# A two-layer encoder step with Strassen-style products: the seam reordered, scalings and squares spread, other final banks, and low halves made five steps ahead

## What is computed

```python
def swiglu(x, g, w_gate, w_up, w_down):
    n = rms_norm(x, g)
    return (jax.nn.silu(n @ w_gate) * (n @ w_up)) @ w_down
...
xp = xp + mix_output(o_a, o_lat, w_uv[l], gn_a[l], gn_b[l], w_out[l])
xp = xp + swiglu(xp, ffn_norm[l], w_gate[l], w_up[l], w_down[l])
...
y_prompt = rms_norm(xp, final_norm)
```

## Time and profile before

| | us |
|---|---|
| median of 3 executions | 1423.65 |
| lowest, highest | 1423.54, 1425.45 |
| the profiled execution | 1426.02 |
| its span, first to last instruction | 1424.7 |

### The profile page before, as it was taken

How to read it: one execution, slowest core, us unless ns; L and a number is a source line. 1 busy time by engine, 2 the same in 40 slices (tenths; PEclk the granted TensorE clock), 3 DMA queues, 4 the chain that set the end, 5 groups by cost and what they waited for, 6 DMA issues and landing times.

```text
span 1424.7 us, 24573 instructions
## 1 busy us (share of the span) xinstructions
PE 1395.9 (98%) x9278; PEld 1313.8 (92%) x9278; DVE 1118.9 (79%) x2032; ACT 737.8 (52%) x1490; POOL 157.6 (11%) x109
## 2 busy tenths in 40 slices
PE   7998999999999999999999999999999999999998
PEld 6887878999999999999988878699999999999998
DVE  5658667878789989988955776677787898988986
ACT  5459555334455455455555675633434544544555
POOL 3415020210000000000062241002000000000002
PEclk9999999999999999999999999999999999999999
DMA  5340221233022222322233211213221223222222
GB/s 172 110 116 12 74 71 35 85 104 104 30 89 66 89 85 74 104 90 75 75 99 108 71 56 47 77 45 119 60 75 60 82 79 107 78 71 90 89 68 97
DMA packets 142372, 115.27 MB, mean 81 GB/s; under 512 B 17808, under 2 KB 136976, under 8 KB 142224
## 3 DMA queue, kind: packets, MB, share of 16 engines
q1 hardware_dynamic: 142256, 113.71, 26.1%
HBM read 108.90 MB, written 6.62 MB: 81 GB/s over the span
## 4 chain that ended last, share of the span: by engine, by line
PE 84%; DVE 8%; ACT 3%; issue 2%; DMA 2%; SPq 1%; DVEq 0%; ACTq 0%
PE ps L692 18%; PE ps L1375 14%; PE ps L1376 14%; PE ps L1377 14%; PE ps L818 3%; PE ps L820 3%; PE ps L819 3%; PE ps L1252 1%; PE ps L1143 1%; ACT pw L1511 1%; DMA wraw<-w_uq 1%; PE ps L742 1%; DVE ringl L2536 1%; PE ps L933 1%; PE ps L1169 1%
## 5 line engine op out<-in xcount | busy, mean ns | idle before, releaser
L1881 ACT ACTIVATE ringh<-sums 128x512 fp32r<-128x512 f32 (+1 forms) x240 | 140.7, 586 | 130.3 <-DVE sums L2527 52.1
L1376 PE MATMUL ps<-tl,ringh 128*128 128x320 f32 x576 | 178.1, 309 | 0.0
L1375 PE MATMUL ps<-tth,ringh 128*128 128x320 f32 x576 | 177.3, 308 | 0.0
L1377 PE MATMUL ps<-tth,ringl 128*128 128x320 f32 x576 | 177.2, 308 | 0.0
L1375 PE MATMUL ps<-dhi,ringh 128*128 128x320 f32 x504 | 158.4, 314 | 6.7 <-DVE xT L2571 3.7
L2536 DVE TENSOR_TENSOR ringl<-sums,ringh 128x512 fp32r<-128x512 f32 (+1 forms) x240 | 152.7, 636 | 7.7 <-ACT ringh L1881 6.4
L1377 PE MATMUL ps<-dhi,ringl 128*128 128x320 f32 x504 | 156.4, 310 | 0.0
L2067 DVE TENSOR_TENSOR wlo<-wraw,whi 128x1024 fp32r<-128x1024 f32 (+1 forms) x69 | 79.6, 1154 | 78.1 <-ACT whi L1463 78.0
L1376 PE MATMUL ps<-dlo_rest,ringh 128*128 128x320 f32 x432 | 134.2, 311 | 0.0
L1376 PE MATMUL ps<-tbl,ringh 128*128 128x320 f32 x432 | 133.5, 309 | 0.0
L1377 PE MATMUL ps<-tbh,ringl 128*128 128x320 f32 x432 | 133.4, 309 | 0.0
(11 more groups left out here) (430 smaller groups left out, 3748.8 us busy)
## 6 DMA issues: line engine op xcount, KB each, us to landing
raw_gate<-w_gate SPq DMA_DIRECT2D x18, 1024.0 KB, 5.4
raw_up<-w_up SPq DMA_DIRECT2D x18, 1024.0 KB, 5.4
raw_gate<-w_down SPq DMA_DIRECT2D x12, 768.0 KB, 4.2
raw_up<-w_down SPq DMA_DIRECT2D x12, 768.0 KB, 4.2
wraw<-w_out SPq DMA_DIRECT2D x32, 128.0 KB, 2.9
wraw<-w_out SPq DMA_DIRECT2D x16, 256.0 KB, 3.1
wraw<-w_gate SPq DMA_DIRECT2D x8, 512.0 KB, 3.8
wraw<-w_up SPq DMA_DIRECT2D x8, 512.0 KB, 3.8
```

Source lines behind the costliest of these rows:

```text
L1375: mm(o, wh[:, c, :], xh[:, c, :], start=fresh and c == 0, stop=False, skip_group_check=True)
L1376: mm(o, wh[:, c, :], xl[:, c, :], start=False, stop=False, skip_group_check=True)
L1377: ins = mm(o, wl[:, c, :], xh[:, c, :], start=False, stop=c == (DP if down else KH) - 1, skip_group_check=True)
L1881: run(ring_of(n, x)[0], left_of(n, x), ACT.Copy).then_inc(a_hi.sem, 1)
```

## The change

Five edits, listed here as the diff has them:

- the first down group of each block runs its products in the order 1, 5, 4, 6, 3, 7, 2 instead of 1, 5, 4, 6, 3, 2, 7; its ScalarE copies `k1` and `k5` are written ahead of the right-hand pieces of the last up group (under that group's product 7), `k2s` under its product 4; the pair of pieces 5 to 7 is made as two pieces, so that there are seven pieces and not six;
- the scalings and squares of the last layer are spread over products 6, 3, 2, 7 of a group (two of them and then two more under 6 and 2 in the last group);
- other banks for the final turns and sums, and half of the turns of tile 2 ahead of the last two products;
- `AHEAD` is 5 instead of 4; `HIGH_AHEAD` stays 5 and `RING` stays 6.

```diff
-AHEAD = 4
+AHEAD = 5
 HIGH_AHEAD = 5
 RING = 6
...
-        for x in (3, 2, 7) if n < NG + NDOWN - 1 else (2, 7, 4, 3):
+        for x in (3, 7, 2) if n == first else (3, 2, 7) if n < NG + NDOWN - 1 else (2, 7, 4, 3):
...
-RIGHT_COUNT = {1: 1, 5: 2, 6: 3, 3: 4, 2: 5, 7: 6, 4: 6}
+RIGHT_COUNT = {1: 1, 5: 2, 6: 3, 3: 4, 7: 5, 2: 6, 4: 7}
...
-        return (6, 0, 4, 6, 0)[t]
+    def y_bank(t, right=0):
+        return ((6, 7), (0, 1), (2, 4), (6, 7), (0, 1))[t][right]
...
                     y_turn(1, range(4))
+                    y_turn(2, range(4))
...
-        y_turn(2, range(8)).then_inc(tile_turned.sem, 1)
+        y_turn(2, range(4, 8)).then_inc(tile_turned.sem, 1)
...
+            def down_copied(n, x):
+                bx, by, bz = group_banks(n)
+                gate_last = GROUPS_OF[(n - NG) // KH + 1][1] - 1
+                act.wait_ge(a_used.sem, a_used.at(l, STEP[n, x] + 1))
+                act.wait_ge(c_new.sem, c_new.at(l, C_NEW[gate_last, {1: 2, 5: 7, 6: 3}[x]]))
+                out, bank = {1: (k1, bx), 5: (k5, by), 6: (k2s, bx)}[x]
+                run(out[:, :], ps[:, bank, 0:HALF], ACT.Copy).then_inc(kept.sem, 1)
...
                     elif x == 7 and final:
+                        down_copied(NG + KH * (n // 6), 1)
+                        down_copied(NG + KH * (n // 6), 5)
                         down_right_hi(pair, 2, 3, t12[:, 1:2, :], right_new, sums + 2)
                         down_right_hi(pair, 4, 5, tu[:, 1:2, half(1)], right_new, sums + 2)
+                        down_right_hi(pair, 5, 6, t34[:, 0:1, :], right_new, sums + 3)
                     elif x == 7:
                         down_right_hi(pair, 1, 3, t12[:, :, :], right_new, sums + 1)
                     elif final:
+                        down_copied(NG + KH * (n // 6), 6)
                         down_right_hi(pair, 3, 4, tu[:, 1:2, half(0)], up_c21, pair + 1)
-                        down_right_hi(pair, 5, 7, t34[:, :, :], right_new, sums + 3)
+                        down_right_hi(pair, 6, 7, t34[:, 1:2, :], right_new, sums + 4)
...
-                if x == 6 and n > NG + 2 * KH:
-                    for c in (2 * (n - NG - 2 * KH) - 2, 2 * (n - NG - 2 * KH) - 1):
-                        if l == DEPTH - 1:
-                            gained(c)
-                            squared(c)
+                if n > NG + 2 * KH and l == DEPTH - 1:
+                    c = 2 * (n - NG - 2 * KH) - 2
+                    if x == 6:
+                        gained(c)
+                    elif x == (3 if n < NG + NDOWN - 1 else 2):
+                        squared(c)
+                        if n == NG + NDOWN - 1:
+                            gained(c + 1)
+                            squared(c + 1)
+                    elif x == 2:
+                        gained(c + 1)
+                    elif x == 7 and n < NG + NDOWN - 1:
+                        squared(c + 1)
...
                 elif g == 0 and x == 5:
                     down_right_lo(q, 4, 4, 5, tu[:, 1:2, half(1)])
+                    down_right_lo(q, 5, 5, 6, t34[:, 0:1, :])
                 elif g == 0 and x == 6:
-                    down_right_lo(q, 6, 5, 7, t34[:, :, :])
+                    down_right_lo(q, 7, 6, 7, t34[:, 1:2, :])
```

More of the change, by code:

```diff
@@ L153 @@
 RIGHT_OF = {1: 0, 5: 1, 6: 2, 2: 3, 3: 4, 7: 5, 4: 6}
-RIGHT_COUNT = {1: 1, 5: 2, 6: 3, 3: 4, 2: 5, 7: 6, 4: 6}
+RIGHT_COUNT = {1: 1, 5: 2, 6: 3, 3: 4, 7: 5, 2: 6, 4: 7}
 def pieces_before(pair):
-    return 4 * pair + pair // DP * 2
+    return 4 * pair + pair // DP * 3
 def right_sums_before(pair):
-    return 2 * KH + 2 * pair + pair // DP
+    return 2 * KH + 2 * pair + pair // DP * 2
 def row_done(d):
@@ L507, in scores_bank @@
         return 5 if n < 2 else 2 * (n % 2)
-    def y_bank(t):
-        return (6, 0, 4, 6, 0)[t]
+    def y_bank(t, right=0):
+        return ((6, 7), (0, 1), (2, 4), (6, 7), (0, 1))[t][right]
     def x_turn_bank(t, right):
@@ L704, in y_turn @@
             for c in chunks:
-                ins = turn(ps[:, y_bank(t) + c // 4, (c % 4) * P:(c % 4 + 1) * P], yT[:, c, tok(t)], ident)
+                ins = turn(ps[:, y_bank(t, c // 4), (c % 4) * P:(c % 4 + 1) * P], yT[:, c, tok(t)], ident)
             return ins
@@ L1420, in square_sums @@
             return ins
+        pe.wait_ge(d_new.sem, d_new.at(DEPTH, -1))
         pe.wait_ge(n_hi.sem, n_hi.at(DEPTH, 0))
@@ L1428, in _ @@
         for t in range(2):
-            ins = square_sums(2, t, [ssq, sq[:, 0], sq[:, 1]])
+            ins = square_sums(3, t, [ssq, sq[:, 0], sq[:, 1]])
         ins.then_inc(stat_sum.sem, 1)
@@ L1432, in _ @@
         for t in range(2, NT):
-            ins = square_sums(3, t, [ssq, sq[:, 0], sq[:, 1]])
+            ins = square_sums(5, t, [ssq, sq[:, 1], sq[:, 0]])
         ins.then_inc(stat_sum.sem, 1)
@@ L1892, in emptied @@
                 if n >= NG:
[L1893 to L1898, removed]
                     return
@@ L2047, in _ @@
         act.wait_ge(stat_sum.sem, stat_sum.at(DEPTH, 1))
-        run(sd[:, 0:2], ps[:, 2, 0:2], ACT.Sqrt, bias=eps, scale=1.0 / D).then_inc(stat_sd.sem, 1)
+        run(sd[:, 0:2], ps[:, 3, 0:2], ACT.Sqrt, bias=eps, scale=1.0 / D).then_inc(stat_sd.sem, 1)
         act.wait_ge(stat_r.sem, stat_r.at(DEPTH, 1))
@@ L2052, in _ @@
         act.wait_ge(stat_sum.sem, stat_sum.at(DEPTH, 2))
-        run(sd[:, 2:NT], ps[:, 3, 2:NT], ACT.Sqrt, bias=eps, scale=1.0 / D).then_inc(stat_sd.sem, 1)
+        run(sd[:, 2:NT], ps[:, 5, 2:NT], ACT.Sqrt, bias=eps, scale=1.0 / D).then_inc(stat_sd.sem, 1)
         act.wait_ge(stat_r.sem, stat_r.at(DEPTH, 2))
@@ L2581, in down_emptied @@
                     down_right_lo(q, 4, 4, 5, tu[:, 1:2, half(1)])
+                    down_right_lo(q, 5, 5, 6, t34[:, 0:1, :])
                 elif g == 0 and x == 6:
-                    down_right_lo(q, 6, 5, 7, t34[:, :, :])
+                    down_right_lo(q, 7, 6, 7, t34[:, 1:2, :])
             def first_rights(n, x):
                 if n >= NG and (n - NG) % KH == 0 and x == 6:
-                    down_right_lo(DP * ((n - NG) // KH) + DP - 1, 5, 3, 4, tu[:, 1:2, half(0)])
+                    down_right_lo(DP * ((n - NG) // KH) + DP - 1, 6, 3, 4, tu[:, 1:2, half(0)])
                 elif n < NG and n % 2 and x == 7:
@@ L2653, in emptied @@
                         vec.tensor_tensor(t12[:, 1, :], tu[:, 1, half(1)], t12[:, 0, :], ALU.subtract).then_inc(right_new.sem, 1)
-                        vec.tensor_tensor(t34[:, 0, :], tu[:, 1, half(1)], tu[:, 0, half(1)], ALU.subtract)
+                        t3 = vec.tensor_tensor(t34[:, 0, :], tu[:, 1, half(1)], tu[:, 0, half(1)], ALU.subtract)
+                        if final:
+                            t3.then_inc(right_new.sem, 1)
                 elif x == 4 and up:
@@ L2660, in emptied @@
                     vec.tensor_tensor(tu[:, 1, half(0)], ps[:, bx, 0:HALF], tg[:, 1, half(0)], ALU.mult).then_inc(up_c21.sem, 1)
-                    dve.wait_ge(right_new.sem, right_new.at(l, right_sums_before(pair) + 1 + final))
+                    dve.wait_ge(right_new.sem, right_new.at(l, right_sums_before(pair) + 1 + 2 * final))
                     dve.wait_ge(up_c21.sem, up_c21.at(l, pair + 1))
@@ L2764, in y_right_half @@
             dve.wait_ge(tile_turned.sem, 2 * NT + t + 1)
-            vec.tensor_scalar(yout[:, t, 512:D], ps[:, y_bank(t) + 1, :], rs[:, t:t + 1], None, ALU.mult).then_inc(y_dve.sem, 1)
+            vec.tensor_scalar(yout[:, t, 512:D], ps[:, y_bank(t, 1), :], rs[:, t:t + 1], None, ALU.mult).then_inc(y_dve.sem, 1)
         dve.wait_ge(stat_sd.sem, stat_sd.at(DEPTH, 1))
```

## The result

The changed kernel takes 1460.05 us (median of four runs, 1458.78 to 1460.76) beside 1424.55 for the kernel before on the same chip: a ratio of 1.0249, 95% interval [1.0237, 1.0260], so 35.5 us slower. The profiled execution has a span of 1458.3 us against 1424.7.

The account below looks back on a forecast made before the run. PE, busy 1395.9 of 1424.7 us, bounds the kernel; VectorE idling over 2.1 us per pair makes it wait. 26.2 + 7.8 - 2.0 - 0.5 = +31.5 us, 1455 against the median; range 1434 to 1468, 8 of 10.

Parts of the forecast that it names:

- Edit 1: Low halves five ahead: VectorE idles 4.3 us per gate/up pair at gate 2, 7 and up 7, 4; 26.2 us slower.
- the 2.1: Gate/up pair: VectorE's spare time in us, 22.48 busy of 24.60; idling beyond it makes PE wait.
- "In plain down groups ... nothing": Down groups: ScalarE answers nothing there, so the high half is ready when VectorE wants it; no cost.
- Edit 2: New order at the seam: six copy waits go, but VectorE idles 1.36 us for a high half; 7.8 us slower.
- Edit 3: Last block's scalings and squares spread: VectorE idles 1.4 instead of 2.0 us, in three groups; -2.0, between -4.3 and +1.
- edit 4: Other banks and earlier turns at the end: same PE work, 0, between -0.4 and +0.4.
- The rule on VectorE and GpSimd: Last block: five GpSimd additions may each hold VectorE, up to 8 us, sum nearer +37; rows kept, about 1 us.
- Rival 3: Gate/up pairs: each PE wait also lowers the clock, 1.7 us each, 20 more, 1475 us; chance 0.06.
- Rivals 1 and 2: First: waits hidden, edits 2 and 3 win, 1413 us, chance 0.06. Second: half hidden, 1435 us, chance 0.16.
- Rival 4: The distance does nothing because of the ring of six; only seam and last block act, about 1424 us; chance 0.04.
- the 1.7 us that the prediction charged to that wait: Last block: after PE's 2.6 us wait the granted clock is 0.57 over 4 us, costing 1.7 us.

Follow-up runs that it names:

- e3: Changed kernel with high halves six steps ahead, ring of seven and t34 moved, low halves still five ahead: 1425.80 us, ratio 1.0011.
- e4: Kernel before with high halves four steps ahead instead of five, low halves staying at four: 1449.22 us, ratio 1.0177.
- e2: Kernel before with low halves five steps ahead instead of four and nothing else: 1461.51 us, ratio 1.0274.
- e7: Kernel before with only the last block's scalings and squares spread over the steps: 1421.36 us, ratio 0.9977.
- e1: Changed kernel with low halves four steps ahead again instead of five: 1421.76 us, ratio 0.9984.
- e11: Changed kernel at four ahead, with the last block's scalings and squares together as before: 1426.01 us, ratio 1.0011.
- e12: Changed kernel at four ahead, low halves of the last hidden pair's seven pieces on 8 of 320 columns in each layer's second and third block: 1417.28 us.
- e8: Changed kernel with GpSimd adding only 8 of 640 columns in the last layer's sums of squares: 1459.75 us, ratio 1.0243.
- e9: Changed kernel with low halves three and high halves four steps ahead, instead of five and five: 1421.55 us, ratio 0.9976.

## Why the prediction was right

**Sign, mechanism and size held**: 1455 forecast, 1460 measured, inside 1434 to 1468.

- **Edit 1** (26.2 forecast): 12 pairs x 2.28 = 27.4 us, at the four named places. Two of its terms were each off by 0.7 us in the same direction, so that the difference held: VectorE idles 0.93 + 0.76 + 0.73 + 1.06 + 0.15 = 3.6 us per pair, not 4.3, and only 3.6 - 2.3 = 1.3 us of it found cover, not the 2.1 that span less busy time had suggested. That the two cancelled is luck, and the 2.1 hangs on where the window is cut: over the same 24.60 us VectorE is busy 22.48 us in rows 3 but 21.08 from 505.51 on, shown above, which would give 3.5. (12 x 2.2 is 26.4, not 26.2.) The cause as stated, the step between high and low half, is shown by e3 and e4.
- **"In plain down groups ... nothing"** failed in part. Its reason held: ahead of the last block, in the stretches from product 6 of the second down group to product 6 of the fourth, no low half waits for a high half. But the first of these stretches (second to third down group) took 9.34 to 10.44 us instead of 9.24 to 9.50, and from product 6 of the second group on, the down groups ahead of the last block together cost 2.0 us where -0.5 was forecast. In the longest of them VectorE meets a sum that waits 1.4 us for the landing of a `w_down` block, and PE waits behind it; but the rows of that wait, before and after, do not grow in total:

```profile
DVE sums L2521 <- DMA raw_gate<-w_down: 3.7, 4, 1.1
```

```profile
DVE sums L2538 <- DMA raw_gate<-w_down: 3.3, 3, 1.4
```

  The earlier step alone does not do it: in e2, with that step and the old seam, the same five stretches took 9.24 us four times and 9.63 once; e7, with neither, has up to 10.08 there, and e3, with five ahead, the new seam and the distance kept, 9.34 to 10.23. The cause of these 2.0 us stays open. In the last block the term does have a price that was put at nothing: with edit 1 alone (e2) its two stretches take 24.5 us instead of 22.9.
- **Edit 2** (7.8 forecast): 6.9 us in the profile, with 1.27 us of idle where 1.36 was worked out, and PE late at the two products named. The price is edit 1's, not the new order's: with the old order at five ahead the six seams cost 9.2 us (e2), so the new one takes 2.3 off. What the step got wrong is the sentence that as written for the old distance it is a gain of up to 6 x 1.0: at four ahead it is 6 x 0.1 (e1, e11), since VectorE's work bounds the seam (e12). In the sum for five ahead that did not matter.
- **Edit 3** (-2.0, between -4.3 and +1): -3.3 alone (e7). In the changed kernel the last block's three parts took 11.51, 10.46 and 8.51 us instead of 12.30, 10.64 and 8.07, only 0.5 less together. (The third part runs from product 6 of the last group to the end of its last product; it is 0.4 to 0.6 longer in e1 and e11 too, which have edit 4's turns, and 0.1 in e7, which has not.) Beside e2, where edit 1 stands alone, the first two parts take 2.5 us less, so the term itself was about right; what the sum lacked is the 1.5 us that edit 1 costs there. The wait of 2.6 us and the low clock are gone as said: in e7 the clock is 1.00 over the four us from 1394, in the changed kernel over the four from 1426. But that the spreading removed the low clock is not shown: e11 keeps the wait (2.7 us) and has no low clock either (last section).
- **The rule on VectorE and GpSimd** that was weighed against the rows: the Trainium skill (SBUF — State Buffer, Who interferes with whom) lets the first of the two hold the other for a whole instruction, and the trace agrees: three of five additions held a VectorE instruction for about 1 us each (1.5 instead of 0.55), and none did in e8. The sum "nearer +37" is nearer to the 35.5 measured, but not for that reason: making the additions small took 1.6 us off two stretches in the profile and 0.3 us off the median.
- **Edit 4** (0): with the seam, nothing beyond what one run varies (e11). **Rival 3**: the clock stays at 1.00 through the pairs. **Rivals 1 and 2**: the idle per pair was above the cover, so neither came. **Rival 4**: the constant alone makes all of the difference (e1, e2).

In the profile the span grew by 33.6 us where the sum says 31.5: the pairs 27.4 (forecast 26.2), the seams 6.9 (7.8), the down groups ahead of the last block 2.0 (-0.5), the last block -0.5 (-2.0) and the end of the kernel behind it 0.7 (0), less 2.9 us in the rest, nearly all of it in stages that the change does not touch and that vary more than that between runs (the start of the first layer's products lies at 372.7 us in e2 and at 377.5 in e1). That these 2.9 us hid part of the excess is luck as well.

## What to carry to other kernels

Where two engines work through fixed lists and hand pieces to each other, look at the distance between the lists, not at how far ahead either is: here one step was right at three and four ahead and 0.3% slower at five (e3), none made the one engine wait inside every hand-over, two made the other wait for what it gets back. Before moving one list, write down all that binds it (here the high half, the sum and the load), in both directions. And a wait that is removed from a stretch bounded by an engine's work comes back at that engine's next product: measure whether less work shortens the stretch before reordering it. Of the versions that compute the whole result the best are the changed kernel with the distance kept at three and four (e9, 0.9976) and the spread scalings alone (e7, 0.9977); they and e1 (0.9984) are not told apart.

## What the runs showed that I had not expected

The same kind of wait of PE was followed by different clocks. In the kernel before, PE is busy 1.36 of 4 us during its wait and the granted clock in the next 4 us is 0.57, most of them at the lower of its two levels; in e11, where scalings and squares stand together as before, it is busy 1.29 of 4 us and the clock stays at 1.00, the upper of its levels, in both stretches. The kernel before, then e11:

```profile
1390.00:1394.00 4.00, 1.36 (x10) 1.10 (x9) 4.00 (x8) 1.47 (x3) 0.79 (x1) 1.00 0.38 122
```

```profile
1386.00:1390.00 4.00, 1.29 (x10) 1.02 (x8) 3.44 (x6) 1.87 (x5) 1.55 (x1) 1.00 0.13 35
1390.00:1394.00 4.00, 4.00 (x27) 3.99 (x28) 4.00 (x10) 1.59 (x4) 0.00 (x0) 1.00 0.48 166
```

So the 1.7 us that the prediction charged to that wait are not a fixed price of it. At the end of the kernel the mean clock differs too (0.85 before, 0.62 after the change, 0.89 in e1 by the same view of the last 11 to 12 us), with no wait of the change near it; what decides it was not tried.
